# A two-layer encoder trunk on one core: expert sums that begin with the scaled residual, the gate row taken a block at a time, and a LayerNorm read from PSUM

## The reference, cut to what matters

```python
for l in range(DEPTH):
    mod = (c_act @ w_ada[l] + b_ada[l])[:, None, :]
    sh1, sc1, g1, sh2, sc2, g2 = jnp.split(mod, 6, axis=-1)
    h = x * (1 + sc1) + sh1
    y = ...                                   # convolution (l = 0) or attention (l = 1)
    x = layer_norm(ALPHA * x + (1 + g1) * y, ln_mix_g[l], ln_mix_b[l])
    h = x * (1 + sc2) + sh2
    y = grouped_moe(h, router_w, router_b, w_gate[l], w_up[l], w_down[l])
    x = layer_norm(ALPHA * x + (1 + g2) * y, ln_ffn_g[l], ln_ffn_b[l])
```

## Time and profile before

| | us |
|---|---|
| median of 3 runs | 1413.11 (1410.93 to 1413.52) |
| profiled execution, its own time | 1413.42 |
| its span, first to last instruction | 1411.7 |
| PE busy | 1138.5 (81%) |
| DVE busy | 412.7 (29%) |
| ACT busy | 188.6 (13%) |
| moved from HBM | 492.20 MB, mean 349 GB/s |
| mean granted TensorE clock | 0.896 |

### The profile page before, as it was taken

One profiled execution on the slowest core, in us unless ns is written; L12 is line 12 of the kernel. 1 busy time (PEld: TensorE's weight loads), 2 busy tenths in 40 slices (PEclk: granted clock), 3 DMA queues, 4 the chain that ended last, 5 costly groups with the idle time before them and its releaser, 6 DMA issues.

```text
span 1411.7 us, 30701 instructions
## 1 busy us (share of the span) xinstructions
PE 1138.5 (81%) x13016; PEld 655.9 (46%) x13016; DVE 412.7 (29%) x1320; ACT 188.6 (13%) x447; POOL 28.0 (2%) x67
## 2 busy tenths in 40 slices
PE   4799998776999569866999888786699996796656
PEld 1586443333555235433565674353356652453333
DVE  0289236111333112311430431551123231131205
ACT  0101221000111001100110331220011110010001
POOL 3020000000000000000000000000000000000000
PEclk8699987888999879977989999788799998998887
DMA  9906969999999999999993131879999799999980
GB/s 373 378 5 276 423 276 426 422 423 427 424 394 425 423 424 428 424 426 423 416 416 152 60 120 60 356 309 425 423 425 416 312 413 425 426 423 423 425 341 30
DMA packets 49298, 494.73 MB, mean 350 GB/s; under 512 B 4239, under 2 KB 4255, under 8 KB 9004
## 3 DMA queue, kind: packets, MB, share of 16 engines
q1 hardware_dynamic: 48176, 490.75, 83.3%
q10 hardware_dynamic: 700, 2.36, 0.4%
q0 software_dynamic: 320, 0.16, 0.1%
HBM read 492.20 MB, written 1.05 MB: 349 GB/s over the span
## 4 chain that ended last, share of the span: by engine, by line
PE 51%; DMA 39%; DVE 6%; ACT 2%; issue 1%; SPq 0%; DVEq 0%; POOLq 0%
DMA ring<-in_w_up_dram 21%; PE PS L1008 21%; DMA ring<-in_w_gate_dram 15%; PE PS L915 6%; PE PS L1124 4%; DMA ring<-in_w_pw_dram 3%; PE PS L832 3%; PE PS L1036 2%; PE PS L987 2%; PE PS L933 2%; PE PS L1230 2%; DVE xs L1359 1%; PE PS L999 1%; PE PS L1277 1%; ACT work L652 1%
## 5 line engine op out<-in xcount | busy, mean ns | idle before, releaser
L1008 PE MATMUL PS<-ring,work 128*32 128x256 f32 x8064 | 524.0, 415 | 166.9 <-DMA ring<-in_w_gate_dram 71.6
L1008 PEld LDWEIGHTS PS<-ring,work 128*32 128x32 f32 x8064 | 278.8, 118 | 394.2 <-issue 126.3
L1526 DVE TENSOR_TENSOR work<-work,PS 128x256 f32<-128x256 f32 x47 | 19.8, 421 | 548.9 <-PE PS L1008 548.0
L915 PE MATMUL PS<-ring,work 128*128 128x512 f32 x192 | 83.1, 593 | 0.5 <-ACT work L784 0.5
L832 PE MATMUL PS<-ring,cact 128*32 128x512 f32 x448 | 64.3, 730 | 20.9 <-DMA ring<-in_w_ada_dram 20.9
L1008 PE MATMUL PS<-work 128*32 128x256 f32 x960 | 63.7, 410 | 20.6 <-DMA work<-in_w_up_dram 12.5
L1124 PE MATMUL PS<-work,ring 128*128 128x256 f32 x256 | 64.0, 415 | 7.7 <-DMA ring<-in_w_pw_dram 6.2
L987 PE MATMUL PS<-hs,work 128*32 128x256 f32 x784 | 59.7, 425 | 11.5 <-DVE work L1494 10.6
L1600 DVE SCALAR_TENSOR_TENSOR work<-work,colv 128x256 f32<-128x256 f32 x150 | 64.1, 484 | 1.2
L652 ACT ACTIVATE work<-PS 128x256 f32<-128x256 f32 x49 | 18.8, 384 | 322.9 <-PE PS L987 322.9
L1124 PEld LDWEIGHTS PS<-work,ring 128*128 128x128 f32 x256 | 52.9, 209 | 18.4 <-DMA ring<-in_w_pw_dram 8.5
(11 more groups left out here) (239 smaller groups left out, 872.2 us busy)
## 6 DMA issues: line engine op xcount, KB each, us to landing
ring<-in_w_gate_dram SPq DMA_DIRECT2D x64, 2048.0 KB, 30.5
ring<-in_w_up_dram SPq DMA_DIRECT2D x54, 2048.0 KB, 29.2
ring<-in_w_down_dram SPq DMA_DIRECT2D x54, 2048.0 KB, 31.0
ring<-in_w_ada_dram SPq DMA_DIRECT2D x24, 2048.0 KB, 18.9
work<-in_w_up_dram SPq DMA_DIRECT2D x10, 2048.0 KB, 29.4
work<-in_w_down_dram SPq DMA_DIRECT2D x10, 2048.0 KB, 28.0
ring<-in_w_pw_dram SPq DMA_DIRECT2D x6, 2048.0 KB, 39.4
ring<-in_w_ada_kv_dram SPq DMA_DIRECT2D x4, 2048.0 KB, 15.0
```

Of the source, the lines that this page charges most:

```text
L915: last = pe.matmul(PS[:, banks + 2 * t + q, :], rows[:, k, t * P:(t + 1) * P], quarter(index + h, kk, KH)[:, q * BANK:(q + 1) * BANK], sta ...
L1008: last = pe.matmul(dst[SLOTS * s:SLOTS * (s + 1), :], rows[:, cc, SLOTS * q:SLOTS * (q + 1)], quarter(load + h, kk, KH)[:, QUART * s:QUART ...
```

## The change

- After the shared rows of a layer are ready, four small matmuls (`spread_g2`) spread (1 + g2) so that partition 32q + s holds quarter q, 256 columns. ACT copies that to a new tile `g2b` (`keep_g2`). PE waits for the copy before it begins the experts.
- The copy of `y_ps` to `yb` moves from ACT to DVE, and becomes a multiply by `g2b`.
- ACT begins the four banks of sums with ALPHA x instead of zeros.
- At the close of an expert half the sums in PSUM are then ALPHA x + (1 + g2) y. ACT's two copies, the spread of g2, the multiply and the add go; statistics are taken from PSUM in eight parts of 256 columns; the norm reads PSUM. Between layers, DVE norms the first 512 columns of both token tiles and ACT the last 512.
- The closes after the convolution and after attention stay as they are, but for `negm`, which now has two columns.

```diff
+            def keep_g2(l):
+                act.wait_ge(g2_spread, l + 1)
+                act.activation(g2b, PS[:, (7, 6)[l], BANK - QUART:BANK], ACT.Copy).then_inc(g2_kept, 1)
             def layer_norm_root(groups=None):
                 l, of_moe = divmod(norms[0] // TT, 2)
-                if of_moe:
-                    act.wait_ge(sums_done, STRIPS * (l + 1))
-                else:
+                if not of_moe:
                     act.wait_ge(y_ready, l + 1)
...
                 if groups is not None:
                     copy_cols(7, groups)
+                if norms[0] == 0:
+                    keep_g2(0)
...
                     act.wait_ge(shift_ready, norms[0] // TT)
-                    act.activation(chunks(hs, 1), by_chunk(xs[:, 1, :]), ACT.Identity, bias=negm[:, 0:1],
+                    if of_moe:
+                        for t in range(TT):
+                            last = act.activation(hs_chunks(t, 1), sums_chunks(t, 1), ACT.Identity, bias=negm[:, t:t + 1],
+                                                  scale=rstd[:, t:t + 1])
+                        last.then_inc(n_half, 1)
+                        return
+                    act.activation(chunks(hs, 1), by_chunk(xs[:, 1, :]), ACT.Identity, bias=negm[:, 1:2],
                                    scale=rstd[:, 1:2]).then_inc(n_half, 1)
...
                 def result_of(n, j):
                     act.wait_ge(hhT_kept, n + 1)
+                    act.wait_ge(yb_copied, n)
                     act.activation(hhT.rearrange("p c s -> p (c s)"), hhT_all[:, bass.ds(j * QUART, QUART)],
                                    ACT.Copy).then_inc(hhT_copied, 1)
-                    act.wait_ge(down_done, n)
-                    act.activation(yb, y_ps, ACT.Copy).then_inc(yb_copied, 1)
...
                 for b in range(4):
-                    act.activation(PS[:, b, :], ones[:, 0:1].to_broadcast([P, BANK]), ACT.Copy,
-                                   scale=0.0).then_inc(sums_zeroed, 1)
+                    act.activation(PS[:, b, :].rearrange("p (t n) -> p t n", t=TT), xs[:, :, b * QUART:(b + 1) * QUART],
+                                   ACT.Copy, scale=ALPHA).then_inc(sums_begun, 1)
...
             copy_hT(acol[:, OF_FFN1, 0, :], acol[:, OF_FFN1, 1, :], 4)
+            keep_g2(1)
             moe(1)
...
+            def spread_g2(tile, l):
+                for q in range(STRIPS):
+                    r, first = 64 + 32 * (q // 2), QUART * (q % 2)
+                    last = pe.matmul(PS[32 * q:32 * q + 32, (7, 6)[l], BANK - QUART:BANK], ones[r:r + 1, 0:32],
+                                     tile[r:r + 1, 2, first:first + QUART], start=True, stop=True,
+                                     tile_position=(r, 32 * q), skip_group_check=True)
+                last.then_inc(g2_spread, 1)
...
                 pe.wait_ge(routed, l + 1)
+                pe.wait_ge(g2_kept, l + 1)
...
             spread_mod(modv[0], 2, 4)
+            spread_g2(modv[0], 0)
             columns(7, ((modv[0], 1), (modv[0], 2)))
...
             moe(L_MOE0, 0)
-            spread_mod(modv[0], 5, 4)
             columns(7, ((modkv, 0), (modv[1], 0)))
...
             turn_n(3)
+            spread_g2(modv[1], 1)
             moe(L_MOE1, 1)
-            spread_mod(modv[1], 5, 4)
             spread_ln(2, 6)
...
             def close_sublayer(ada_next=None, done=None):
+                if of_moe:
+                    dve.wait_ge(sums_done, STRIPS * (l + 1))
+                    for t in range(TT):
+                        for q in range(STRIPS):
+                            last = dve.bn_stats(stats[:, t, q, :], sums(t, q))
+                else:
...
                 if done is None:
-                    dve.scalar_tensor_tensor(out=negm[:, 0:1], in0=mv[:, 1, 0:1], scalar=-1.0, in1=rstd[:, 1:2],
+                    dve.scalar_tensor_tensor(out=negm[:, :], in0=mv[:, :, 0], scalar=-1.0, in1=rstd[:, :],
                                              op0=ALU.mult, op1=ALU.mult).then_inc(shift_ready, 1)
+                    if of_moe:
+                        for t in range(TT):
+                            last = dve.tensor_scalar(hs_chunks(t, 0), sums_chunks(t, 0), mv[:, t, 0:1], rstd[:, t:t + 1],
+                                                     ALU.subtract, ALU.mult)
+                        last.then_inc(h_ready, 1)
+                        add_ada(*ada_next, 6)
+                        return
...
                 for t in range(TT):
-                    last = dve.tensor_scalar(xs[:, t, :], xs[:, t, :], mv[:, t, 0:1], rstd[:, t:t + 1],
+                    last = dve.tensor_scalar(xs[:, t, :].rearrange("p (b n) -> p b n", b=STRIPS),
+                                             PS[:, 0:STRIPS, QUART * t:QUART * (t + 1)], mv[:, t, 0:1], rstd[:, t:t + 1],
                                              ALU.subtract, ALU.mult)
...
                     dve.wait_ge(late_on, n)
                     build_GW(n + 1)
+                    dve.wait_ge(down_done, n)
+                    dve.tensor_tensor(yb, y_ps, g2b, ALU.mult).then_inc(yb_copied, 1)
```

More of the change, by code:

```diff
@@ L156, in trunk_kernel @@
         eps = sb("eps", [P, 1])
-        negm = sb("negm", [P, 1])
-        stats = sb("stats", [P, TT, 2, 6])
+        negm = sb("negm", [P, TT])
+        stats = sb("stats", [P, TT, STRIPS, 6])
         mv = sb("mv", [P, TT, 2])
@@ L202, in trunk_kernel @@
         r_gt = part(2 * GROUPS * PER * PER, to="p (r i j) -> p r i j", i=PER, j=PER)
+        g2b = part(QUART)
         assert at[0] <= 7168 + KD * SEQ - EXTRA * KH * D
@@ L345, in trunk_kernel @@
         yb_copied = sem("yb_copied")
+        g2_spread = sem("g2_spread")
+        g2_kept = sem("g2_kept")
         k_done = sem("k_done")
@@ L388, in by_chunk, with sums_chunks, hs_chunks @@
             return a.rearrange("s (h p k) -> s h k p", h=2, k=KH)
+        def sums_chunks(t, h):
+            tile = PS[:, 2 * h:2 * h + 2, QUART * t:QUART * (t + 1)]
+            return tile.rearrange("s b (p k) -> s b p k", k=KH)
+        def hs_chunks(t, h):
+            tile = hs[:, t, h * HALF:(h + 1) * HALF]
+            return tile.rearrange("s (k b p) -> s b p k", b=2, k=KH)
         def chunks(tile, t):
@@ L620, in layer_norm_root @@
                 l, of_moe = divmod(norms[0] // TT, 2)
-                if of_moe:
-                    act.wait_ge(sums_done, STRIPS * (l + 1))
-                else:
+                if not of_moe:
                     act.wait_ge(y_ready, l + 1)
-                for t in range(TT):
-                    if of_moe:
-                        if STRIPS == 4:
-                            y, dst = PS[:, 0:STRIPS, QUART * t:QUART * (t + 1)], hs[:, t, :].rearrange("p (b n) -> p b n", b=STRIPS)
-                        else:
-                            y, dst = PS[:, 2 * t:2 * t + 2, :].rearrange("p b n -> p (b n)"), hs[:, t, :]
-                    else:
-                        y, dst = PS[:, 2 * t:2 * t + 2, :].rearrange("p b n -> p (b n)"), hs[:, t, :]
-                    act.activation(dst, y, ACT.Copy).then_inc(y_read, 1)
+                    for t in range(TT):
+                        act.activation(hs[:, t, :], PS[:, 2 * t:2 * t + 2, :].rearrange("p b n -> p (b n)"),
+                                       ACT.Copy).then_inc(y_read, 1)
                 if groups is not None:
                     copy_cols(7, groups)
+                if norms[0] == 0:
+                    keep_g2(0)
                 for t in range(TT):
@@ L1372, in close_sublayer @@
             def close_sublayer(ada_next=None, done=None):
+                l, of_moe = divmod(ys[0], 2)
                 ys[0] += 1
-                row = spread_banks(4)
-                for t in range(TT):
-                    dve.wait_ge(y_read, 2 * (ys[0] - 1) + t + 1)
-                    last = dve.tensor_tensor(hs[:, t, :], hs[:, t, :], row, ALU.mult)
-                last.then_inc(spread_used, 1)
-                dve.wait_ge(spread_used, spreads[0])
-                for t in range(TT):
-                    last = dve.scalar_tensor_tensor(out=xs[:, t, :], in0=xs[:, t, :], scalar=ALPHA, in1=hs[:, t, :],
-                                                    op0=ALU.mult, op1=ALU.add)
+                parts_of = STRIPS if of_moe else 2
+                if of_moe:
[4 more added lines that the diff above has]
+                else:
+                    row = spread_banks(4)
+                    for t in range(TT):
+                        dve.wait_ge(y_read, TT * l + t + 1)
+                        last = dve.tensor_tensor(hs[:, t, :], hs[:, t, :], row, ALU.mult)
+                    last.then_inc(spread_used, 1)
+                    dve.wait_ge(spread_used, spreads[0])
+                    for t in range(TT):
+                        last = dve.scalar_tensor_tensor(out=xs[:, t, :], in0=xs[:, t, :], scalar=ALPHA, in1=hs[:, t, :],
+                                                        op0=ALU.mult, op1=ALU.add)
+                    link(last)
```

(9 more changed lines are left out.)

9 lines of the change are left out of this document (5 added, 4 removed).

## The result

In the first comparison, eight runs of each kernel, the changed kernel took a median of 1404.9 us (1401.2 to 1409.1) and the kernel before 1412.0 (1407.8 to 1413.8): ratio 0.995, 95% interval 0.9934 to 0.9967. That is faster, as forecast, but 1404.9 lies under the range of 1406.0 to 1412.1. Three more comparisons held a copy of the changed kernel. Over all four, 37 runs of it have a mean of 1405.25 (standard deviation 3.7, from 1398.1 to 1412.0) and 109 runs of the kernel before 1411.07 (2.0). The difference is -5.8 us, 95% about -7.1 to -4.6 if every run counts by itself. The four comparisons one by one, by means against their own runs of the kernel before, gave -7.1, -3.9, -6.1 and -7.2; taken as four values they have a mean of -6.1 and an interval of about -8.5 to -3.6. So the gain is shown, its size only to some 2 us.

The account below looks back on a forecast made before the run. PE and DMA carry nine tenths of the final path; PE binds the close after layer 0, ACT and DVE the last. Terms 0.58 + 0 + 0 + 0.36 - 0.78 - 4.6 = -4.4 took 1413.4 to 1409.0 us, range 1406.0 to 1412.1.

Parts of the forecast that it names:

- entry of layer 0: Ahead of layer 0's experts, the gate row's four added matmuls delay PE and the weight stream: +0.58 us.
- entry of layer 1: Ahead of layer 1's experts, the gate row's spread fits a PE wait of 1.08 us: 0, at most +0.6.
- seed: ACT's four writes starting the sums read x instead of a constant: 0, upper bound 2.3 us.
- product of a block: A block's result becomes a DVE product instead of an ACT copy, delaying PE at nine waits: +0.36 us.
- close after layer 0: After layer 0's experts PE binds and loses the spread of g2: -0.78 us; DVE's shorter path stays covered.
- last close: After layer 1's experts the ACT and DVE chain gets shorter: net -4.6 us, bounds -6.0 and -3.5.
- 1413.4 - 4.4 = 1409.0: Whole kernel: the profiled execution's time less the summed terms gives the forecast of 1409.0 us.
- A: Whole kernel: small costs take most of the gain, no measurable change; 1412.1 or about 1411 us; chance 0.24.
- B: Both closes pay: DVE's 5 us count after layer 0 too, or ada there runs at full clock, 1406.3; chance 0.09.
- C: Slower by TensorE's clock: both adas, before and after layer 0's experts, at half clock throughout, 1417.7 us; chance 0.05.
- D: In every repeated block the DVE product holds PE, needing DVE 1.5 us late; its chance counted in A.
- Adas with another clock: A sign that would show the forecast wrong: adas running at another clock than before; no size given.

Follow-up runs that it names:

- layer 1 alone: The changed kernel with the new forms only in layer 1 and layer 0 as in the kernel before; ratio 0.9969 to the kernel before, mean -4.4 us.
- ada first: The changed kernel with the ada before layer 0's experts put ahead of the gate row's spread and the columns; ratio 0.9971 to the kernel before.
- spread x7: The changed kernel with the spread of the gate row ahead of layer 0's experts done seven times; ratio 0.999 to the kernel before.

## Why the prediction was right and wrong

**The terms of the sum, one by one.**

| term | forecast | measured | from |
|---|---|---|---|
| entry of layer 0 | +0.58 | +0.56 to +1.01 itself; +0.7 in the stream | below |
| entry of layer 1 | 0 | 0 | turn to router 4.75 and 4.51, before 4.68 and 4.64 |
| seed | 0 | 0 | L686 0.582 |
| product of a block | +0.36 | 0.04 to 0.05 x 9 | L1580, layer 1 alone |
| close after layer 0 | -0.78 | -0.86 | three profiles before, all of after |
| last close | -4.6 | -4.51 | 7.72 against 12.23 |
| sum | -4.4 | about -4.3 | |

Every term held to some 0.15. Within the last close two sizes were off and cancelled in part: the statistics 2.75 instead of 8 x 0.36 + 0.06 = 2.94 and the norm +1.07 instead of +0.82. At layer 0's entry the spread starts 0.56 to 0.79 ahead of the columns in five profiles and 0.98 to 1.01 in four, which is the same eight instructions at a lower clock; after is one of the four (190.65 - 189.67 = 0.98).

**The step that failed** is the line "1413.4 - 4.4 = 1409.0", at both of the things that it takes for granted beside the terms.

First its base. 1413.4 is one execution, 0.3 above a median of three; the mean of 109 runs of the kernel before is 1411.07. Of the 4.1 us between 1409.0 and 1404.9, 2.3 are this. From 1411.1 the same sum gives 1406.7, inside the range, and the range moved by 2.3 would be 1403.7 to 1409.8 and hold 1404.9. This is a mis-sized term and not a mechanism.

Second, it puts at nothing what PE's clock does in the stretches that the change doesn't touch. The mean over 37 runs is 5.8 under before, 1.4 more than the sum. (The last 0.4 are that the first comparison's median of 1404.9 lies under the mean of all four, 1405.25.) By the interval over the four comparisons, -8.5 to -3.6, the 1.4 could be chance. What the profiles do show is how a stretch without an edit comes to differ, in two places.

*Layer 0's entry.* Waits of PE for weights in layer 0 end on a grid of 4.9 us, one load each, so the stream's delay can be read at one such wait, that for the second half of the up weights near 341 us. PE's path from there to the 6th combine is short and has no wait for DMA. Before:

```profile
336.51 3.64 PE L1008 MATMUL PS<-work 128*32 128x256 f32 x32 [3.90 <-DMA work<-in_w_up_dram]
...
341.41 3.64 PE L1008 MATMUL PS<-ring,work 128*32 128x256 f32 x32 [1.26 <-DMA ring<-in_w_up_dram]
...
348.14 3.66 PE L1008 MATMUL PS<-ring,work 128*32 128x256 f32 x64 [0.97 <-DVE work L1516]
```

After:

```profile
336.01 3.21 PE L1032 MATMUL PS<-work 128*32 128x256 f32 x32 [2.42 <-DMA work<-in_w_up_dram]
...
340.92 1.93 PE L1032 MATMUL PS<-ring,work 128*32 128x256 f32 x32 [1.70 <-DMA ring<-in_w_up_dram]
...
345.63 3.66 PE L1032 MATMUL PS<-ring,work 128*32 128x256 f32 x64 [0.98 <-DVE work L1557]
```

And before, in its second execution:

```profile
335.60 1.93 PE L1008 MATMUL PS<-work 128*32 128x256 f32 x32 [1.28 <-DMA work<-in_w_up_dram]
...
340.49 3.36 PE L1008 MATMUL PS<-ring,work 128*32 128x256 f32 x32 [2.96 <-DMA ring<-in_w_up_dram]
```

The same 32 instructions behind the wait take 3.64, 1.93 and 3.36. The windows of 6 us from there on have the granted clock, before and after:

```profile
341.40:347.40 6.00, 5.68 (x52) 2.61 (x52) 0.62 (x2) 0.77 (x2) 0.00 (x0) 0.66 1.02 423
```

```profile
340.90:346.90 6.00, 4.94 (x76) 2.78 (x80) 2.31 (x9) 0.77 (x2) 0.00 (x0) 1.00 1.01 422
```

Over all profiles, counted from the spread of g1:

| entry | profiles | landing | landing to 6th combine | clock there |
|---|---|---|---|---|
| old | 3 | 151.98 to 152.31 | 30.80 to 31.13 | 0.66 to 0.72 |
| new | 4 | 152.24 to 152.81 | 30.74 to 30.84 | 0.72 to 0.73 |
| new | 5 | 152.93 to 153.29 | 29.15 to 29.17 | 1.00 |
| ada first | 1 | 153.26 | 29.15 | 1.00 |
| spread x7 | 1 | 158.29 | 30.85 | 0.72 |

So the entry costs what was forecast, +0.7 on the mean of landings (152.88 against 152.14). But in five of nine profiles the strips that follow ran at full clock and gave 1.7 back: net -0.3 on the mean, where +0.58 was summed. The half clock was not spared in those five. The 32 strips ahead of the wait took 3.2 to 3.6 there, against 1.93 in the other four, in the seven spreads and in two of the three old ones, and PE then waited 1.3 to 1.7 for the weights instead of 3.0: it fell where PE would have waited for the weights anyway, and cost nothing that shows. The seven spreads, +6.1 at the landing against the old entry and +5.4 against the mean of the new one, show the same path from the other side. The five are those in which the new spread itself was slowest (0.79 to 1.01), so the executions part ways already there. That the later landing goes with the half clock lying ahead of it is what the rows of the unedited entries show (with seven spreads the landing is later still, and the half clock behind it); what puts it there is not settled.

*Behind layer 0's close.* From the closing combine of layer 0 to the first combine of layer 1 the old close took 239.4, 239.2 and 237.7 in three profiles. The new close took 235.0 to 240.2 in nine, mean 237.2. On the means that is -1.5, of which -0.86 is the spread of g2. One piece, in which no line of the change is at work, is the spread of layer 0's LayerNorm rows (L857, now L872). Before, in its second execution:

```profile
729.33 3.90 PE L857 MATMUL PS<-lnrows,ones 1*128 1x512 f32 x8
```

and after:

```profile
726.10 2.33 PE L872 MATMUL PS<-lnrows,ones 1*128 1x512 f32 x8
```

All profiles with the new close have 2.3 to 2.4 here, two of three with the old one 3.7 and 3.9. The third, layer 1 alone, has 2.3, so this is a matter of the execution also, and the rest of -1.5 (0.6 in a scatter of 2 us either way) is not shown to be the change's. With these two places (-0.3 for +0.7, and -0.6 more) the terms would make -4.3 - 1.0 - 0.6 = -5.9, close to the -5.8 of the runs, but that closeness is luck. By the same means the other stretches moved too: -0.6 ahead of the spread of g1, where no line differs, +0.2 in layer 0's experts and -0.3 in layer 1's. All six rows together make -7.0 in the profiles. So the mean of 3 and 9 to 11 profiles can't say where 1.4 us come from, and their cause stays open.

Layer 1's experts show how far such a stretch can go. Over the fourteen profiles they took 452.9 to 457.2. All four of the changed kernel lie at 456.1 to 457.2, all six of its edited copies at 452.9 to 453.9, and layer 1 with the old forms had 455.8, 455.9 and 453.4; yet none of the edits has a line at work there.

**The range** was too narrow for a second reason: its scatter came from three runs of the kernel before, 2.6 us wide. The changed kernel's runs have a standard deviation of 3.7 against 2.0, and medians of 6 to 12 runs came out between 1401.4 and 1408.3. The median of 1404.9 is within that. The stretches above at 29.2 or 30.8, 323.8 or 326.2 and 235 to 240 make up a good part of it. The 323.8 or 326.2 is mainly the 32 strips at 1.93 or 3.64 behind the last awaited weights. Why the changed kernel spreads more is open.

**The rivals.** A, that small costs eat the gain: out, since the handover cost 0.05 and neither the seed nor the reads cost more than the sum had. B: its first form is out by the 3.2 to 3.6 us that DVE and ACT had to spare. Its second, ada at full clock, is the direction in which it went: ada behind the new close took 8.3 to 8.8 against 9.74 and 9.55. But it needed hardly any of the shorter DVE path: combine to turn was 14.35 in layer 1 alone, with the old close and an ada of 8.66, and the old path of DVE and ACT was ready at 13.2, where the new close turned at 13.2 to 13.6. The prediction's "5 us" for that path was 3.4, since it left out that the root waits at this close for the copy of the columns and the table load. C, slower by the clock: the opposite sign at this close; at the entry, however, ada did take longer in five of the nine profiles (9.66 to 9.98 against 8.95 in the earlier trace rows), the same five in which later strips ran at full clock; in the other four it took 8.4 to 8.7. D didn't occur.

**What was to show it.** The statistics start 0.14 behind combine (1387.09 against 1386.95), L916 follows L847, the tiles are normed 3.6 us before the turn and not 4, combine is 0.55 behind the strips, and the DMA share at the same place in layer 1's experts is 0.45 and 0.50 in two profiles against 0.53: right, or right but for 0.4. "Adas with another clock" stood among the signs of a wrong forecast, and it was the one that came.

## What to carry to other kernels

Folding a scale and a residual into sums that PSUM accumulates anyway pays where a chain of DVE and ACT steps closes the kernel, and there alone: the same edit at a close that PE binds gave the 0.9 us of PE's own work and none of the 3.4 by which DVE's and ACT's path became shorter. Start such a sum from the mean of many runs and not from the execution that was profiled: that alone was 2.3 us here, half of the effect. Price by rows the steps on the path that ends last, then ask by how much the stretches without any edit differ between two executions of the kernel before; that scatter, and not the bounds of the terms, sets the width of a range for an effect of 0.3%. Where a kernel alternates between the two clock levels, cut the profiles at landmarks before comparing totals, and look which side of an awaited load a slow stretch lies on: ahead of it, it was free here; behind it, it cost 1.7 us.

## What was not expected of the hardware

- The granted clock moved whole stretches without any edit of them: 32 strips in 1.93 or 3.64 us, 16 instructions of the attention in 3.72 or 6.75, and 235.0 to 240.2 us for one stretch under one close.
- A table load on ACT (1.28 us) starts right behind the activation before it. It cost nothing at the last close while ACT waited for DVE, and 0.8 us once one copy of 1.02 stood ahead of it. At layer 0's close, behind the copy of the columns, it kept the root 2.1 us behind a finished aggregate.
- A norm of 1024 columns read from PSUM takes 1.30 a tile, more than an addition of two operands one of which is in PSUM (2.35 the pair, 1.18 each); a subtract and multiply with a second tensor (scalar_tensor_tensor) from PSUM takes 1.24. Fusing the gain into it cost DVE nothing.
